# First mixture: weight chunks as single pieces of 2 MB, and a narrow class of tiles with 72 columns

## What is computed

```python
def moe_swiglu(u, w_router, wg, wu, wd):
    bsz, seq, d = u.shape
    xf = u.reshape(bsz * seq, d)
    logits = (xf @ w_router).astype(F32)
    vals, idx = lax.top_k(logits, TOP_K_EXPERTS)
    w = jax.nn.softmax(vals, axis=-1)
    gate = jnp.sum(jax.nn.one_hot(idx, N_EXPERTS, dtype=F32) * w[..., None], axis=1)
    y = jnp.zeros_like(xf)
    for e in range(N_EXPERTS):
        y = y + gate[:, e:e + 1].astype(xf.dtype) * swiglu(xf, wg[e], wu[e], wd[e])
    return y.reshape(bsz, seq, d)
```

## Time and profile before

| | us |
|---|---|
| median of 3 runs | 2075.75 |
| lowest, highest run | 2075.08, 2092.02 |
| profiled execution, as a run | 2082.44 |
| its span | 2080.4 |
| first mixture, L754 first to last | 701.4 to 1575.5 |
| mean granted TensorE clock | 0.968 of full speed |

### The profile page before, as it was taken

How to read it: one execution, slowest core, us unless ns; L and a number is a source line. 1 busy time by engine, 2 the same in 40 slices (tenths; PEclk the granted TensorE clock), 3 DMA queues, 4 the chain that set the end, 5 groups by cost and what they waited for, 6 DMA issues and landing times.

```text
span 2080.4 us, 70905 instructions
## 1 busy us (share of the span) xinstructions
PE 1938.5 (93%) x32806; PEld 1704.7 (82%) x32807; DVE 572.8 (28%) x1309; ACT 445.3 (21%) x886; POOL 24.7 (1%) x44
## 2 busy tenths in 40 slices
PE   7879999999999999999999999999999999778988
PEld 4668888888557899999999999999998787656666
DVE  2687733341452401000010101010104253411222
ACT  3351000042653211111111111111113422311112
POOL 0000000000010000000000000000000000000000
PEclk9999999999899899999999999999999989899999
DMA  9617878734464598998999999999995213385895
GB/s 399 234 64 283 348 312 330 287 121 162 192 247 190 204 384 346 390 391 354 423 398 422 403 422 400 422 399 423 404 423 214 81 42 121 131 354 242 339 411 238
DMA packets 68328, 621.58 MB, mean 299 GB/s; under 512 B 7584, under 2 KB 7840, under 8 KB 8480
## 3 DMA queue, kind: packets, MB, share of 16 engines
q1 hardware_dynamic: 64224, 566.80, 67.2%
q0 software_dynamic: 3456, 50.33, 5.9%
q10 hardware_dynamic: 576, 3.42, 0.4%
HBM read 619.47 MB, written 1.05 MB: 298 GB/s over the span
## 4 chain that ended last, share of the span: by engine, by line
PE 74%; DMA 17%; DVE 4%; ACT 3%; issue 1%; SPq 0%; DVEq 0%; POOL 0%; ACTq 0%; POOLq 0%
PE psum L754 28%; DMA ring<-in_moe_w_up 11%; PE psum L552 9%; DMA ring<-in_w_up 4%; PE psum L836 4%; PE psum L651 4%; PE psum L668 4%; PE psum L677 4%; PE psum L740 2%; PE psum L886 2%; PE psum L507 1%; PE psum L531 1%; PE psum L1272 1%; DMA ring<-in_w_ada.0 1%; PE psum L813 1%
## 5 line engine op out<-in xcount | busy, mean ns | idle before, releaser
L754 PE MATMUL psum<-uT,ring 128*64 128x80 f32 (+1 forms) x14336 | 545.6, 237 | 14.2 <-DMA ring<-in_moe_w_up 11.5
L754 PEld LDWEIGHTS psum<-uT,ring 128*64 128x64 f32 x14336 | 528.6, 137 | 26.9 <-DMA ring<-in_moe_w_up 18.3
L754 PE MATMUL psum<-arena,ring 128*64 128x80 f32 (+1 forms) x7168 | 270.5, 236 | 2.4 <-issue 1.9
L754 PEld LDWEIGHTS psum<-arena,ring 128*64 128x64 f32 x7168 | 264.8, 137 | 2.7 <-issue 2.1
L1859 DVE TENSOR_TENSOR arena<-arena,psum 128x288 f32<-128x288 f32 x56 | 25.4, 454 | 691.0 <-PE psum L754 691.0
L1459 ACT ACTIVATE arena<-psum 128x384 f32<-128x384 f32 x56 | 27.5, 490 | 662.5 <-PE psum L754 662.5
L836 PE MATMUL psum<-ring,uT 128*32 128x128 f32 x3584 | 110.7, 286 | 34.1 <-DMA ring<-in_w_up 19.0
L836 PEld LDWEIGHTS psum<-ring,uT 128*32 128x32 f32 x3584 | 104.8, 115 | 45.9 <-DMA ring<-in_w_up 20.5
L1690 DVE SCALAR_TENSOR_TENSOR arena<-ring,cact,arena 128x512 f32<-128x512 f32 x168 | 126.3, 752 | 5.7
L552 PE MATMUL psum<-uT,ring 128*128 128x256 f32 (+1 forms) x496 | 112.5, 388 | 11.2 <-ACT arena L1355 9.3
L552 PEld LDWEIGHTS psum<-uT,ring 128*128 128x128 f32 (+1 forms) x496 | 94.8, 193 | 27.6 <-issue 8.4
(11 more groups left out here) (432 smaller groups left out, 1817.1 us busy)
## 6 DMA issues: line engine op xcount, KB each, us to landing
ring<-in_moe_w_gate SPq DMA_DIRECT2D x112, 1024.0 KB, 9.4
ring<-in_moe_w_up SPq DMA_DIRECT2D x112, 1024.0 KB, 9.4
ring<-in_moe_w_down SPq DMA_DIRECT2D x112, 1024.0 KB, 10.6
ring<-in_w_ada.0 SPq DMA_DIRECT2D x12, 2048.0 KB, 17.3
ring<-in_w_ada.1 SPq DMA_DIRECT2D x12, 2048.0 KB, 14.0
ring<-in_w_ada SPq DMA_DIRECT2D x12, 2048.0 KB, 9.2
ring<-in_w_up SPq DMA_DIRECT2D x8, 2048.0 KB, 14.1
ring<-in_w_down SPq DMA_DIRECT2D x8, 2048.0 KB, 11.4
```

The costliest lines, as they stand in the source:

```text
L754: mm = pe.matmul(out(HD * hc), w[:, c0 + HD * hc:c0 + HD * hc + HD], x, skip_group_check=True, **kw)
```

## The change

Each weight of a chunk is loaded by one DMA of 2 MB instead of two of 1 MB. `Mix` gets three landing semaphores instead of six, and `few` = 72 instead of 80. TensorE waits once for each weight (before k = 0, and before f = 0 in down) instead of twice. It still raises `M.g`, `M.u` and `M.dn` twice a chunk; SP waits for the second of the two and then issues the whole piece of the next chunk. The order gate, up, down on SP stays.

```diff
--- before.py
+++ after.py
@@ -227,7 +227,7 @@
                 self.clA, self.clV = sem(f"{tag}_cleared_low"), sem(f"{tag}_cleared_high")
                 self.ytA, self.ytV, self.tr = sem(f"{tag}_sums_low"), sem(f"{tag}_sums_high"), sem(f"{tag}_transposed")
 
-        mix = [Mix("m1", E1, F1, 96, 6, posi[:, 0:64], 80), Mix("m2", E2, F2, 64, 6, posi[:, 64:192], 0)]
+        mix = [Mix("m1", E1, F1, 96, 3, posi[:, 0:64], 72), Mix("m2", E2, F2, 64, 6, posi[:, 64:192], 0)]
         by_token = sq.rearrange("p a n -> p (a n)").rearrange("p (t n) -> p t n", t=NT)
         res = sem("results")
         act_took = sem("act_took"); dve_took = sem("dve_took")
@@ -769,16 +769,16 @@
                     with pe.Fori(0, CH) as c:
                         n = q * CH + c
                         for k in range(KT):
-                            if k % 4 == 0:
-                                pe.wait_ge(M.land[k // 4], n * 16 + 16)
+                            if k == 0:
+                                pe.wait_ge(M.land[0], n * 16 + 16)
                             for f in range(4):
                                 mm = block(lambda r: psum[r:r + HD, 0, N * f:N * f + W], wg[:, k, :], M.xg[:, k, 0:W], P * f,
                                            start=(k == 0 and f == 0), stop=(k == KT - 1))
                             if k % 4 == 3:
                                 mm.then_inc(M.g, 1)
                         for k in range(KT):
-                            if k % 4 == 0:
-                                pe.wait_ge(M.land[2 + k // 4], n * 16 + 16)
+                            if k == 0:
+                                pe.wait_ge(M.land[1], n * 16 + 16)
                             for f in range(3):
                                 mm = block(lambda r: psum[r:r + HD, 1, N * f:N * f + W], wu[:, k, :], M.xg[:, k, 0:W], P * f,
                                            start=(k == 0 and f == 0), stop=(k == KT - 1))
@@ -792,8 +792,8 @@
                         for f in range(4):
                             if f in (0, 3):
                                 pe.wait_ge(M.hid, n * 2 + (1 if f == 0 else 2))
-                            if f % 2 == 0:
-                                pe.wait_ge(M.land[4 + f // 2], n * 16 + 16)
+                            if f == 0:
+                                pe.wait_ge(M.land[2], n * 16 + 16)
                             for k in range(KT):
                                 mm = block(lambda r: psum[r:r + HD, 2 + k // 4, N * (k % 4):N * (k % 4) + W], wd[:, f, :],
                                            M.hidden[:, 0, N * f:N * f + W], P * k, start=False, stop=False)
@@ -2403,25 +2403,22 @@
                 load(n)
             WEIGHTS = ("moe_w_gate", "moe_w_up", "moe_w_down")
 
-            def granule(e, c, i):
+            def granule(e, c, r):
 
                 M = mix[0]
-                r, j = i // 2, i % 2
-                w = A[WEIGHTS[r]][bass.ds(e, 1)][:, c, :, SLOT // 2 * j:SLOT // 2 * j + SLOT // 2]
-                dst = ring[:, M.slots[r], SLOT // 2 * j:SLOT // 2 * j + SLOT // 2]
-                sp.dma_start(dst, w.rearrange("e p n -> p (e n)")).then_inc(M.land[i], 16)
-
-            def granule_used(q, c, i):
+                w = A[WEIGHTS[r]][bass.ds(e, 1)][:, c, :, :]
+                sp.dma_start(ring[:, M.slots[r], :], w.rearrange("e p n -> p (e n)")).then_inc(M.land[r], 16)
+
+            def granule_used(q, c, r):
 
                 M = mix[0]
-                return (M.g, M.u, M.dn)[i // 2], q * (2 * M.CH) + (2 * c + i % 2 + 1)
+                return (M.g, M.u, M.dn)[r], q * (2 * M.CH) + (2 * c + 2)
 
             M = mix[0]
             CH = M.CH
-            for i in range(6):
-                if i % 2 == 0:
-                    sp.wait_ge(*freed[occupant[M.slots[i // 2]]])
-                granule(0, 0, i)
+            for r in range(3):
+                sp.wait_ge(*freed[occupant[M.slots[r]]])
+                granule(0, 0, r)
             for n in names[BEFORE_MOE1:AFTER_MOE1]:
                 load(n)
             sp.wait_ge(s_tab, 1)
@@ -2429,21 +2426,21 @@
             with sp.Fori(0, last) as q:
                 e = sp.value_load(M.tab[0:1, bass.ds(q, 1)], min_val=0, max_val=E1 - 1)
                 for c in range(CH - 1):
-                    for i in range(6):
-                        sp.wait_ge(*granule_used(q, c, i))
-                        granule(e, c + 1, i)
+                    for r in range(3):
+                        sp.wait_ge(*granule_used(q, c, r))
+                        granule(e, c + 1, r)
                 e = sp.value_load(M.tab[0:1, bass.ds(q + 1, 1)], min_val=0, max_val=E1 - 1)
-                for i in range(6):
-                    sp.wait_ge(*granule_used(q, CH - 1, i))
-                    granule(e, 0, i)
+                for r in range(3):
+                    sp.wait_ge(*granule_used(q, CH - 1, r))
+                    granule(e, 0, r)
             e = sp.value_load(M.tab[0:1, bass.ds(last, 1)], min_val=0, max_val=E1 - 1)
             for c in range(CH - 1):
-                for i in range(6):
-                    sp.wait_ge(*granule_used(last, c, i))
-                    granule(e, c + 1, i)
+                for r in range(3):
+                    sp.wait_ge(*granule_used(last, c, r))
+                    granule(e, c + 1, r)
             for r in range(3):
                 occupant[M.slots[r]] = f"first{r}"
-                freed[f"first{r}"] = granule_used(last, CH - 1, 2 * r + 1)
+                freed[f"first{r}"] = granule_used(last, CH - 1, r)
             for n in names[AFTER_MOE1:]:
                 load(n)
 
```

## The result

The changed kernel is slower: ratio 1.0043 to before, 95% interval 1.0031 to 1.0056, so about 9 us (medians 2089.55 against 2079.93 us, 20 runs each). The prediction was 1.9 us slower. It moved the way forecast, by more than was forecast, and stays inside the range of 2068 to 2090 us and inside 1%.

What follows compares the result with a forecast made beforehand. Narrow tiles were taken as bound by the DMA queue: stream 596.6, start 7.2, boundaries 24.5 and tail 9.0 us make 637.3, 1.9 us more than now. Forecast 2077.7 us, range 2068 to 2090.

Steps and rivals of the forecast that it cites:

- What bounds the kernel: Narrow tiles: the DMA queue sets the pace, 14.92 us a chunk at 422 GB/s, 1.6 us above TensorE's own pace.
- The width: Narrow chunks at 72 columns: 4.11 us per 128 instructions, no tile changes class, counting only behind boundaries and at the ends.
- The rate: Weight stream in narrow tiles: whole 2 MB pieces move at 429 GB/s instead of 422, so 14.67 us a chunk.
- Rival 1: Narrow-tile stream: the rate does not follow piece size and stays 422 GB/s; 2086.7 us, chance 0.15.
- Wide tiles: The two wide tiles: refill fits with 2.6 us to spare, so they stay as they are.
- Steady narrow chunks: Within narrow tiles: queue stays full with 2.6 us to spare; TensorE waits 0.78 us before each piece.
- rivals 2, 3 and 4: Narrow tiles: queue holes between pieces, 2114 us (0.09); clock falls, +10 us a chunk (0.03); TensorE bounds, 2034 us (0.03).
- The tile boundary: Between narrow tiles: late refill leaves the queue empty for 4.9 us, where it now loses 2.7.
- the fixed part: Behind a tile boundary: 2.8 us from the request until data moves and is seen, besides the transfer itself.
- The sum: Six narrow tiles: stream, start, five boundaries and tail make 637.3 us against 635.4, 1.9 us more.
- the term of the hole: Empty queue behind each of five boundaries: 4.9 us, kept as 4.2 to 5.7; 24.5 us in all.
- The count's own range: Whole kernel: 2070 us (431 GB/s and the smaller idle) to 2083 us (idle 5.7), around 2077.7; chance 0.70.

Runs made afterwards that it cites:

- halves_72: The kernel before with only the width changed, 72 columns for 80, half pieces of 1 MB kept; ratio 1.0008 to before.
- whole_80: The changed kernel (whole 2 MB pieces) with the width put back from 72 to 80; ratio 1.0072 to before.
- whole_runs8k: The changed kernel with weights laid out by halves, so each 2 MB DMA moves two 8 KB runs per partition; ratio 1.0070 to before.
- up_by_f_72: The kernel before with up's halves cut by inner-column blocks instead of by k, and 72 columns; ratio 0.9967 to before, 0.9980 when run again.

## Why the prediction was right or wrong, point by point

**What bounds the kernel**: right. Narrow tiles run at the queue's speed; halves_72 and the steady chunk of every run show it.

**The width**: the matmul was priced right (256 instructions in 8.22 us, less the last one's duration 4.0 us for 128, against 4.11), no tile changed class, and as said it is worth time only around a boundary. Shown by whole_80 against the changed kernel: 1.1 us a tile.

**The rate**: right, 429 GB/s, and 14.68 us for 14.67. Rival 1 is out. That rows of 512 B already run at line rate (the Trainium skill, DMA: Bandwidth & Descriptors, Specifications) does not hold to the last 1.7% here: whole_runs8k has 422 with 8 KB runs in the same DMAs.

**Wide tiles**: right. 119.9 and 119.6 us clear to clear, 119.4 and 119.3 before.

**Steady narrow chunks**: right. Waits of 0.6 to 0.8 us at each piece, full windows, clock 1.00; rivals 2, 3 and 4 did not happen.

**The tile boundary**: the right mechanism, and the term of the sum that was mis-sized. I counted 4.9 us of empty queue; it is 5.9 by the period. The 16.8 us from the landing of the last down to the request are right (1146.38 to 1163.23). Wrong was the fixed part beside them. I took 2.8 us, from pieces that find the queue empty (7.7 less 4.89), and as long as a piece is alone that holds. These are the loads issued behind one boundary of the changed kernel (median us to landing):

```profile
ring<-in_moe_w_gate SPq DMA_DIRECT2D x1, 2048.0 KB, 7.7
ring<-in_moe_w_up SPq DMA_DIRECT2D x1, 2048.0 KB, 9.5
```

Gate is issued at 1163.23 and lands at 1170.9; up is issued at 1167.08 and lands at 1176.6, 5.7 us behind gate and not 4.89. Up to gate's landing the count holds: 24.5 us from the landing of the last down, for four pieces of 4.89, so 4.9 us are lost. The other 0.8 us are lost between gate and up. (Behind the boundary at 1050 us gate lands later and up 5.1 us behind it; the whole is the same.)

Seen from the traffic: it ran dry about 13.1 us after the last down was seen landed, while 14.68 us of pieces were still to land by my count. So some 1.6 us of them had already moved. Behind the request the traffic is slow at first (201 GB/s over 1163.0 to 1166.5), which loses another 1.6 to 1.9 us. So 3.2 to 3.5 us stand where I had 2.8, and 16.85 + 3.2 to 3.5 - 14.68 gives 5.4 to 5.7 us, just under the 5.9 of the period.

In a full queue a landing is seen later than alone, and the trace shows part of the reason. A DMA raises its semaphore sixteen times, and TensorE goes on with the sixteenth. The trace holds the time of each. For the last down ahead of this boundary the sixteenth came 0.6 us behind the mean of all (0.6 to 1.2 us at the five boundaries), so most of the sixteen parts were done earlier. If each part goes on with the next piece at once, that makes 0.6 of the 1.6 us; the rest is open.

The fixed part of about 2.0 us of the Trainium skill (DMA: Bandwidth & Descriptors, Anatomy of one DMA, given there for GpSimd's path) would have missed by more: 2.8 us for a piece alone, and 0.8 us more for the one behind it, are what this case shows.

**The sum**: the narrow tiles take 643.8 us (941.3 to 1585.1) where 637.3 were forecast and 635.4 were before. Five boundaries at 1.0 us more are 5 of the 6.5 us; the stream's 14.68 to 14.69 for 14.67 is 0.4 to 0.8; the rest is at the start and the tail. The mechanism and its signs (10 us back by the rate, more than that taken by the refill) were right, the term of the hole was 1 us too small, and as two large terms of opposite sign were subtracted, this made 1.9 into 9 us. The count's own range (to 2083) did not reach 1.0043; its bound of 5.7 us for the hole was just short. As that range began at 2070, under the time before, the sign of the forecast was in part luck.

**What stays open**: why at 72 columns with halves cut by k the queue runs low sooner than at 80 (period 107.4 against 106.9), and why up_by_f_72 does not. The times of the sixteen increments point at something that no experiment here varied. Within a tile they keep their distances from piece to piece; from tile to tile these change. "Ahead" is how far the mean of the sixteen was ahead of the last, for the last down in front of a boundary; "lacking" is the traffic that was missing from 3 us before the clear to 20 us behind it, against 422 GB/s. Four boundaries each:

| kernel | ahead, us | lacking, us |
|---|---|---|
| before | 0.6, 1.0, 1.0, 0.4 | 2.3, 2.7, 2.6, 2.0 |
| halves_72 | 2.5, 2.1, 1.6, 1.0 | 4.0, 3.8, 2.4, 1.5 |
| up_by_f_72 | 0.9, 0.4, 0.5, 0.8 | 1.9, 1.4, 1.4, 1.8 |
| up_by_f_72_again | 0.9, 0.7, 1.1, 1.0 | 2.0, 1.4, 2.2, 2.1 |

In halves_72 the hole is the deeper, the further the others were ahead of the last one. That fits a queue that holds less, when TensorE pauses, than the landings say. Where halves_72 was 1.0 us ahead it lacked 1.5 us, no more than up_by_f_72. So the traces do not show that the cut of up saves time by itself. What sets the distances, and whether the change of up had a part in it, is not known.

## What to carry to other kernels

When a stream is bound by the queue, ask of each pause of its reader not how long it is but when it gives the first slot back: the pause plus the use of the first piece plus issue and latency, against what is then still queued, less what has moved of it unseen (1.6 us here). Larger pieces buy rate (here 1.7%, by the longer run per partition, not by fewer DMAs) and pay in refill time at every pause; here seven chunks between pauses give 1.7 us back, and the hole grew from some 2.4 to 5.9 us. Cutting up so that its first half returns at half time made, with 72 columns, the only version faster than before; that it is so because of the earlier return was not shown.

## What the runs showed of the hardware

Runs of 8 KB per partition stream at 422 GB/s in DMAs of 1 and of 2 MB, runs of 16 KB at 429. A landing is seen 2.8 us plus the transfer after issue for a piece alone (7.7 us for 2 MB); the piece behind it was seen 0.8 us later than its transfer accounts for. The sixteen increments of one DMA come spread over 1.1 us in the changed kernel (piece at 1146.24) and over 3.1 us in halves_72 (piece at 1147.20), and keep their distances while the queue is full.

Making TensorE's work cheaper can slow what follows. Behind a scatter of one column in place of 256, the granted clock was 0.66 over the next 5 us in four of six narrow tiles; behind waits of 2.4 us it fell to 0.54 over 2 us some of the time; behind waits of 0.6 to 0.8 us, three in a chunk, it held at 1.00. That activity is what releases the clock is what the Trainium skill says too (TensorE: Matmul & The Clock Gate, Part 1); the trace agrees, and adds that instructions of one column, though the engine counts as busy, did not keep it up in four of six cases (16 of them in 1.92 us).
